# The end of a decoder-layer kernel: a branch decided while the last scatters run, and waits in place of two barriers

## The chip, the cores and the metric

The kernel runs on all eight cores of one Trainium2 chip. The input has eight sequences, and each core computes one of them whole; the cores do not exchange data. The metric is the device time, in microseconds (us), of the slowest core.

## The reference, cut to what matters

The reference is one decoder layer on x of shape (8, 2048, 2048). Three sub-layers add to the residual stream h: a mixer (causal pooling beside an RWKV-7 recurrence), a cross-attention into 256 memory tokens, and a mixture of experts. The last one, and the final norm behind it, are what the end of the kernel computes:

```python
hn = _rmsnorm(h, norm_ffn_g[l])
h = h + _hier_moe(hn, ...)       # top-1 of 4 groups, then top-2 of the 4 experts inside it
return _rmsnorm(h, norm_final_g)
# _hier_moe: for e in range(16):
#     hid = silu(t @ w_gate[e]) * (t @ w_up[e])
#     out = out + gates[:, e:e+1] * (hid @ w_down[e])
```

A token therefore uses two experts of one group, one of the six pairs of that group, and there are 24 such pairs in all.

## The kernel before, in words

The kernel is written as a list of operations per stage. A planner, the class `Sched`, gives each operation a modelled duration and writes them out for five engines in a planned order; `emit` (line 312) turns the order into instructions and places a wait only where an engine does not yet know that an operation is done. Each compute engine has one semaphore that counts its operations. The DMA queues of SP and POOL have 20 semaphores each and use them in turn; each transfer adds 16 to its own.

The stages run in this order: norm and projections, the mixer, cross-attention with the routing of the tokens, and the experts. The expert stage sorts the 2048 tokens of the core into 24 buckets of at most 128 tokens, one for each pair of experts. A bucket is gathered from DRAM by POOL, goes through its two experts, is normed by `finish_bucket`, and is scattered to `out` by POOL with an indirect DMA of 1 MB (line 1395). The last three buckets are finished by expert 15, one after the other: ACT squares the rows, DVE scales them (line 173), POOL issues the scatter.

A bucket holds 128 tokens. If a pair has more, the flag `flgi`, written by DVE before the expert stage begins (line 1305), is 1, and a general path must compute everything once more, tile by tile. The code for it follows the expert stage, inside `with nc.If(fv > 0)` (lines 1459 to 1513). With the present inputs the flag is 0 and the path is skipped: the profile shows none of its compute.

What follows the last scatter, on each of the five engines:

- `S.drain()` (line 1454, the waits themselves on line 372): a wait for every semaphore that is in use, in the order of the list `final`: first the engines' counts, then the DMA semaphores in the order of their first use. There are 43 of them on every engine.
- `nc.all_engine_barrier()` (line 1455): a DRAIN on each engine and an exchange of semaphores through POOL.
- `values_load` (line 1458): each engine loads the flag into a register (TENSOR_LOAD).
- the branch (COMPARE_BRANCH, recorded under line 1513), which jumps over the code of the general path.
- `nc.all_engine_barrier()` (line 1514): a second DRAIN and exchange.

Of the kernel before, what the change touches and what calls it, by code (L numbers as in the profile page):

```python
# [50 lines left out]
class Ring:  # L51
# [3 lines left out]
    def next(self):  # L55
        b = self.b[self.i % len(self.b)]
        self.i += 1
        return b.fresh()
# [9 lines left out]
class Sched:  # L68
# [241 lines left out]
    def emit(self):  # L310
        order = self.schedule()
        self.order = order
        known = {e: {} for e in self.ENG}
        cnt = dict.fromkeys(self.ENG, 0)
        slot_i = dict.fromkeys(self.slots, 0)
        slot_n = {}
        for o in order:
            e = o.eng
            kn = known[e]
            toks = []  # L320
            if o.bytes:
                sl = self.slots[e]
                s = sl[slot_i[e] % len(sl)]
                slot_i[e] += 1
                v = slot_n.get(id(s), (s, 0, None))
                if v[1] > 0:
                    toks.append((v[2].end, s, v[1], v[2].clock))
                slot_n[id(s)] = (s, v[1] + 16, o)
                o.tok = (s, v[1] + 16)
            else:  # L330
                cnt[e] += 1
                o.tok = (self.sem[e], cnt[e])
            for p in o.preds:
                if p.eng == "pe" and e == "pe" and not p.bytes:
                    continue
                toks.append((p.end, p.tok[0], p.tok[1], p.clock))
            toks.sort(key=lambda t: -t[0])
            waits = []
            for _, s, v, ck in toks:
                if kn.get(id(s), 0) >= v:  # L340
                    continue
                waits.append((s, v))
                for k2, v2 in ck.items():
                    if kn.get(k2, 0) < v2:
                        kn[k2] = v2
                if kn.get(id(s), 0) < v:
                    kn[id(s)] = v
            o.clock = dict(kn)
            b = self.b[e]
            if o.pre:  # L350
                for p in o.pre[1]:
                    if p is not None:
                        b.wait_ge(*p.tok)
                o.pre[0](b)
            for s, v in waits[1:]:
                b.wait_ge(s, v)
            r = o.fn(b)
            if not isinstance(r, list):
                r = [r]
            if waits:  # L360
                r[0]._wait_ge(*waits[0])
            r[-1].then_inc(o.tok[0], 16 if o.bytes else 1)
        self.final = [(self.sem[e], cnt[e]) for e in self.ENG if cnt[e]] + [(s, v) for s, v, _ in slot_n.values()]
        self.ops = []

    def all_sems(self):
# [36 lines left out]
def r3(ap, a):  # L403
    return ap.rearrange("p (a b) -> p a b", a=a)
# [19 lines left out]
def build(stop=99, fallback=True):  # L424
    nc = bass.Bass("TRN2", target_bir_lowering=False)  # L425
# [40 lines left out]
    with ExitStack() as es:  # L466
        S = Sched(nc, es)
# [14 lines left out]
        run, tab, tabi, idx, flg, flgi = al.f32(24), al.f32(72), al.f32(48), al.f32(24), al.f32(1), al.f32(1)  # L482
# [30 lines left out]
        def pvc(name, j=0):  # L513
            c = PV[name] + j
            return pv.a[:, c:c + 1]
# [205 lines left out]
        order = [(q, h) for h in range(6) for q in (0, 1)] + [(0, 6), (0, 7), (1, 6), (1, 7), (2, 0), (2, 1), (3, 0), (3, 1)]  # L721
# [244 lines left out]
        if stop >= 2:  # L966
# [7 lines left out]
            for u in range(32 + 2):  # L974
# [7 lines left out]
                if u < 32:  # L982
# [10 lines left out]
                    if u == 0:  # L993
                        for f_ in first:
                            s_, e_, _ = next(r for r in S.regions if r[2] is f_)
# [297 lines left out]
        if stop >= 5:  # L1293
# [126 lines left out]
            for e in range(16):  # L1420
# [14 lines left out]
                for db, j in [(db, j) for db in range(4) for j in range(3)] if e < 15 else [(db, j) for j in range(3) for db in range(4)]:  # L1435
# [5 lines left out]
                    y, yq, _ = bk[b]  # L1441
# [9 lines left out]
                        finish_bucket(b)  # L1451

        S.emit()
        S.drain()
        nc.all_engine_barrier()
        if stop >= 5 and fallback:

            fv = nc.values_load(flgi.a[0:1, 0:1], min_val=0, max_val=1, skip_runtime_bounds_check_because="a comparison gives 0 or 1")
            with nc.If(fv > 0):
                with nc.Fori(0, NTT) as it:  # L1460
                    S2 = Sched(nc, es, "f", dict(sp=4, pool=4, act=1))
                    bank2 = Ring([Buf(psum[:, i * 512:(i + 1) * 512]) for i in range(8)])
                    f_ = Al(S2, big, CONST_W, WORDS)
                    y, xn, XT, gt, hid, sb = f_.f32(D), f_.bf16(D), f_.bf16(D), f_.f32(16), f_.bf16(512), f_.bf16(128)
                    fst, gF2 = f_.f32(8), f_.f32(D)
                    fwr = f_.bf16s(4, 8192)
                    S2.dma("sp", y.a, h2_s[bass.ds(it * 128, 128), :], W=[y])
                    S2.dma("sp", gt.a, gat_s[bass.ds(it * 128, 128), :], W=[gt])
                    S2.dma("sp", gF2.a, gB[3], W=[gF2])

                    def frms():
                        S2.act(xn.a, y.a, AF.Square, R=[y], W=[xn], P=[fst], accum_out=fst.a[:, 0:1])
                        S2.act(fst.a[:, 1:2], fst.a[:, 0:1], AF.Ln, R=[fst], W=[fst], scale=1.0 / D, bias=pvc("epsn"))
                        S2.act(fst.a[:, 2:3], fst.a[:, 1:2], AF.Exp, R=[fst], W=[fst], scale=-0.5)
                    frms()
                    S2.stt(xn.a, y.a, fst.a[:, 2:3], gF2.a, ALU.mult, ALU.mult, R=[y, fst, gF2], W=[xn])
                    for q in range(4):
                        b = bank2.next()
                        S2.mm([(b.a[:, j * 128:(j + 1) * 128], xn.a[:, (q * 4 + j) * 128:(q * 4 + j + 1) * 128], identb.a, True, True) for j in range(4)], R=[xn], W=[b])
                        S2.cp(r3(XT.a, 16)[:, q * 4:q * 4 + 4, :], r3(b.a, 4), R=[b], P=[XT])  # L1480
                    for e in range(16):
                        ws = []
                        for k in range(3):
                            w = fwr.next()
                            for c in range(4):
                                S2.dma("pool", w.a[:, c * 2048:(c + 1) * 2048], wel[k][e][c], P=[w])
                            ws.append(w)
                        for f in range(4):
                            fs = slice(f * 128, (f + 1) * 128)
                            bs = [bank2.next(), bank2.next()]  # L1490
                            for i in range(2):
                                S2.mm([(bs[i].a[:, 0:128], ws[i].a[:, f * 2048 + kc * 128:f * 2048 + (kc + 1) * 128], r3(XT.a, 16)[:, kc, :], kc == 0, kc == 15) for kc in range(16)],
                                      R=[ws[i], XT], W=[bs[i]])
                            S2.act(sb.a, bs[0].a[:, 0:128], AF.Silu, R=[bs[0]], W=[sb])
                            S2.tt(hid.a[:, fs], bs[1].a[:, 0:128], sb.a, ALU.mult, R=[bs[1], sb], W=[hid])
                        for db in range(4):
                            b = bank2.next()
                            ds_ = slice(db * 512, (db + 1) * 512)
                            S2.mm([(b.a, hid.a[:, f * 128:(f + 1) * 128], ws[2].a[:, db * 2048 + f * 512:db * 2048 + (f + 1) * 512], f == 0, f == 3) for f in range(4)], R=[hid, ws[2]], W=[b])
                            S2.stt(y.a[:, ds_], b.a, gt.a[:, e:e + 1], y.a[:, ds_], ALU.mult, ALU.add, R=[b, gt, y], W=[y])  # L1500
                    frms()
                    S2.dma("sp", gF2.a, gB[2], W=[gF2])
                    S2.stt(y.a, y.a, fst.a[:, 2:3], gF2.a, ALU.mult, ALU.mult, R=[y, fst, gF2], W=[y])
                    S2.dma("sp", out[bass.ds(it * 128, 128), :], y.a, R=[y])
                    S2.emit()
                    S2.drain()
                    nc.all_engine_barrier()
                    nums = sorted(s.num for s in S2.all_sems())
                    assert nums[-1] - nums[0] == len(nums) - 1
                    nc.gpsimd.dma_reset(range(nums[0], nums[-1] + 1))  # L1510
                    nc.gpsimd.sem_clear(range(nums[0], nums[-1] + 1))
                    nc.all_engine_barrier()
            nc.end_ifs() if hasattr(nc, "end_ifs") else None
            nc.all_engine_barrier()
    mybir.codegen_inst_isa_subclasses(nc)
    return nc

# [75 lines left out]
```

## Time and profile before

| what | us |
|---|---|
| median of 3 runs | 2406.62 (2404.75 to 2407.84) |
| the profiled execution's own time | 2419.8 |
| its span, first to last recorded instruction, slowest core (core 5) | 2418.2 |
| spans of the other cores | 2385.5 to 2407.6 |

The profile is one execution on the slowest core. The own time is longer than the span, since it also holds what runs ahead of the first recorded instruction and behind the last; no view lists what that is. Times in the rows are counted from the start of the span of their core.
### The profile page before, as it was taken

To read this page: it belongs to the slowest core of one execution; us is meant where nothing else is said; L and a number is where in the kernel's file an instruction comes from. 1 tells how busy PE (TensorE), PEld (TensorE's weight loads), DVE (VectorE), ACT (ScalarE), POOL (GpSimd) and SP (SyncE) were. 2 spreads that over 40 slices of the span, in tenths; PEclk is the share of its full clock that TensorE was granted. 3 is DMA by queue.
4 is the path that set the end of the run, shared out by engine and by line. 5 is a ranking of instruction groups with operands and counts; after the bars stand their busy time and mean duration, and the time that the engine had idled before them with its cause. 6 is when DMAs were issued, how large, how long until landed. Compare 5 with 4: busy or idle time off the path is not lost.

```text
span 2418.2 us, 57666 instructions; the slowest of 8 cores (2385.5 to 2418.2 us)
## 1 busy us (share of the span) xinstructions
PE 2214.5 (92%) x25176; PEld 1264.0 (52%) x25180; DVE 1401.7 (58%) x2734; ACT 1249.3 (52%) x2325; POOL 382.8 (16%) x655
## 2 busy tenths in 40 slices
PE   5899999999889999989997999999999699999995
PEld 3455555555455555545554444455454566655562
DVE  3455667677647666657676334334343567767664
ACT  6655766668677676657776223233232425243333
POOL 3122112221231212311010000000000101111111
PEclk9788999999989999999999999999999699999997
DMA  9689878885886988956775689999999588999983
GB/s 231 98 133 124 107 113 129 128 128 100 138 143 128 151 129 130 141 99 109 121 119 180 145 159 156 160 158 158 167 163 193 184 235 266 284 284 272 278 241 135
DMA packets 178432, 393.80 MB, mean 163 GB/s; under 512 B 59104, under 2 KB 108768, under 8 KB 166400
## 3 DMA queue, kind: packets, MB, share of 16 engines
q0 software_dynamic: 95568, 217.45, 58.0%
q1 hardware_dynamic: 82608, 172.62, 23.3%
q8 instruction: 200, 3.28, 0.6%
q14 instruction: 56, 0.46, 0.1%
HBM read 531.76 MB, written 142.74 MB: 279 GB/s over the span
## 4 chain that ended last, share of the span: by engine, by line
PE 74%; DMA 11%; DVE 7%; ACT 5%; issue 3%; POOL 0%; another core or an unknown queue 0%; POOLq 0%
PE ps L134 74%; ACT big L161 5%; DVE big L168 4%; DVE big L173 2%; DMA big<-wgc 2%; DMA qkd<-big 2%; DMA big<-x 1%; DMA big<-w_kv 1%; DMA big<-w_rkv 1%; DMA big<-w_lo 1%; DMA vod<-big 1%; DMA big<-w_qT 1%; DMA big<-wuc 1%; DVE big L189 1%; DMA big<-h_s,big 1%
## 5 line engine op out<-in xcount | busy, mean ns | idle before, releaser
L134 PE MATMUL ps<-big 64*64 64x64 bf16 (+7 forms) x25176 | 2214.5, 258 | 176.3 <-ACT big L161 69.0
L134 PEld LDWEIGHTS ps<-big 64*64 64x64 bf16 (+3 forms) x25176 | 1263.6, 108 | 1120.2 <-issue 169.3
L161 ACT ACTIVATE big<-ps 128x512 bf16<-128x512 f32 (+2 forms) x922 | 512.4, 591 | 533.5 <-PE ps L134 488.9
L161 ACT ACTIVATE big<-big 128x512 f32<-128x512 f32 (+6 forms) x896 | 546.0, 634 | 432.2 <-DVE big L168 195.2
L168 DVE TENSOR_TENSOR big<-ps,big 128x512 bf16<-128x512 f32 (+3 forms) x664 | 466.2, 714 | 485.7 <-PE ps L134 330.2
L161 ACT ACTIVATE big<-ps,big 128x512 f32<-128x512 f32 (+3 forms) x332 | 213.1, 648 | 179.6 <-PE ps L134 175.6
L173 DVE SCALAR_TENSOR_TENSOR big<-ps,big 128x512 f32<-128x512 f32 (+1 forms) x316 | 224.2, 721 | 107.5 <-ACT big L161 68.4
L173 DVE SCALAR_TENSOR_TENSOR big<-big 128x512 f32<-128x512 f32 (+3 forms) x284 | 237.7, 859 | 32.6 <-ACT big L161 9.8
L168 DVE TENSOR_TENSOR big<-big 128x512 bf16<-128x512 f32 (+12 forms) x412 | 197.7, 503 | 25.5 <-ACT big L161 24.4
L173 DVE SCALAR_TENSOR_TENSOR big<-big,ps 128x64 f32<-128x64 f32 (+1 forms) x280 | 92.6, 332 | 148.1 <-PE ps L134 146.5
L189 DVE CAST big<-ps 128x512 bf16<-128x512 f32 x150 | 100.5, 685 | 31.6 <-ACT big L161 13.0
L203 POOL DMA_DIRECT2D big<-w_kv x128 | 67.9, 539 | 137.8 <-PE ps L134 137.2
L203 POOL DMA_DIRECT2D wuc<-wu_l x64 | 33.5, 523 | 332.5 <-DVE big L168 157.0
L203 POOL DMA_DIRECT2D wdc<-wd_l x64 | 33.7, 527 | 304.6 <-DVE big L168 143.5
L203 POOL DMA_DIRECT2D big<-wg_l x32 | 17.9, 560 | 306.1 <-PE ps L134 306.1
L1230 DVE RECIPROCAL big<-big 128x4 f32<-128x4 f32 x16 | 2.8, 175 | 108.8 <-ACT big L161 108.8
L1395 POOL DMA_INDIRECT out<-big x24 | 30.1, 1254 | 128.2 <-DVE big L173 125.8
L749 DVE TENSOR_TENSOR_SCAN big<-big 128x512 f32<-128x512 bf16 x32 | 39.1, 1221 | 16.3 <-ACT big L161 16.0
L161 ACT ACT_TABLE_LOAD x37 | 47.5, 1283 | 1.7 <-PEq L425 1.1
L203 POOL DMA_DIRECT2D wgc<-wg_l x32 | 16.7, 523 | 191.1 <-DVE big L168 66.2
L203 POOL DMA_DIRECT2D big<-w_o x64 | 34.1, 546 | 73.8 <-PE ps L134 73.4
L203 POOL DMA_DIRECT2D big<-w_rkv x48 | 25.7, 537 | 123.3 <-PE ps L134 122.8
(26 smaller groups left out, 284.5 us busy)
## 6 DMA issues: line engine op xcount, KB each, us to landing
big<-x SPq DMA_DIRECT2D x32, 1024.0 KB, 12.4
wuc<-wu_l POOLq DMA_DIRECT2D x64, 512.0 KB, 10.2
wdc<-wd_l POOLq DMA_DIRECT2D x64, 512.0 KB, 10.4
big<-wuc SPq DMA_DIRECT2D x64, 512.0 KB, 9.4
big<-wdc SPq DMA_DIRECT2D x64, 512.0 KB, 12.9
big<-w_rkv POOLq DMA_DIRECT2D x48, 512.0 KB, 11.8
big<-w_kv POOLq DMA_DIRECT2D x128, 128.0 KB, 5.4
wgc<-wg_l POOLq DMA_DIRECT2D x32, 512.0 KB, 12.6
```

What stands on the lines that cost most here:

```text
L134: r.append(e.matmul(out, lhsT=lhsT, rhs=rhs, start=st, stop=sp_, **k))
L161: return self.op("act", lambda e: e.activation(out=out, in_=in_, func=func, **kw), dur, R, W, P, tbl=TBL.get(func))
L168: return self.op(eng, lambda e: e.tensor_tensor(out=out, in0=a, in1=b, op=op), dur, R, W, P, after=after)
L173: return self.op(eng, lambda e: e.scalar_tensor_tensor(out=out, in0=a, scalar=s, in1=b, op0=op0, op1=op1), dur, R, W, P)
L189: return self.op(eng, lambda e: e.tensor_copy(out=out, in_=a), dur, R, W, P)
L203: return self.op(eng, lambda e: e.dma_start(out=out, in_=in_, **extra), 550.0 if eng == "pool" else 60.0, R, W, P, nbytes=nb, **kw)
L749: S.op("dve", lambda e: e.tensor_tensor_scan(out=tC.a, data0=rmask.a, data1=tS.a, initial=0.0, op0=ALU.mult, op1=ALU.add), 1260.0, R=[rmas ...
L1230: S.op("dve", lambda e, st=st: e.reciprocal(out=st.a[:, 8:12], in_=st.a[:, 4:8]), 100.0, R=[st], P=[st])
L1395: S.op("pool", lambda e: e.indirect_dma_start(out=out, out_offset=IOA(ap=idx.a[:, b:b + 1], axis=0), in_=y.a, in_offset=None, bounds_check ...
```

## The change: what it does

The list `final` is sorted by the time at which the planner expects the last operation behind each semaphore to end. The waits and the barrier ahead of the branch are moved into the general path. In their place each engine waits for the operation that wrote the flag, loads the flag and branches. Behind the branch, in place of the second barrier, stands `S.drain()`: the same 43 waits on every engine, now in the sorted order. Nothing else differs.

```diff
@@ emit
-        self.final = [(self.sem[e], cnt[e]) for e in self.ENG if cnt[e]] + [(s, v) for s, v, _ in slot_n.values()]
+        fin = [(max(o.end for o in order if o.eng == e and not o.bytes), self.sem[e], cnt[e]) for e in self.ENG if cnt[e]]
+        fin += [(o.end, s, v) for s, v, o in slot_n.values()]
+        self.final = [(s, v) for _, s, v in sorted(fin, key=lambda t: t[0])]
@@ build, behind the expert stage
         S.emit()
-        S.drain()
-        nc.all_engine_barrier()
         if stop >= 5 and fallback:
+            for e in S.ENG:
+                S.b[e].wait_ge(*flgi.w.tok)
             fv = nc.values_load(flgi.a[0:1, 0:1], ...)
             with nc.If(fv > 0):
+                S.drain()
+                nc.all_engine_barrier()
                 with nc.Fori(0, NTT) as it:
...
             nc.end_ifs() if hasattr(nc, "end_ifs") else None
-            nc.all_engine_barrier()
+        S.drain()
```

## Rows read from the trace of the kernel before

**Rows 1.** The page: its head, and busy time of the engines.
```profile
span 2418.2 us, 57666 instructions; the slowest of 8 cores (2385.5 to 2418.2 us)
PE 2214.5 (92%) x25176; PEld 1264.0 (52%) x25180; DVE 1401.7 (58%) x2734; ACT 1249.3 (52%) x2325; POOL 382.8 (16%) x655
```

**Rows 2.** Timeline from 2398 us to the end: start, duration, engine, line, operation.
```profile
2396.22 2.35 DVE L173 SCALAR_TENSOR_TENSOR big<-big 128x2048 f32<-128x2048 f32 x1 [0.37 <-ACT big L161]
2398.85 0.98 POOL L1395 DMA_INDIRECT out<-big  x1 [1.75 <-DVE big L173]
```

**Rows 3.** Line 1395 from 2390 us on, the last three scatters: issue to landing.
```profile
DMA to landing us min/median/max: 4.6/4.6/4.6
```

**Rows 4.** Line 372, waits ahead of the first barrier: ns min/median/max, first and last start.
```profile
L372 PEldq EVENT_SEMAPHORE  x43: 51/51/51, 2390.8 to 2405.5; - x43
L372 ACTq EVENT_SEMAPHORE  x43: 13/17/21, 2396.0 to 2404.5; - x43
L372 DVEq EVENT_SEMAPHORE  x43: 21/21/21, 2396.2 to 2404.7; - x43
L372 POOLq EVENT_SEMAPHORE  x43: 4/17/17, 2398.6 to 2404.6; - x43
```

**Rows 5.** Line 372 from 2403.42 us on, behind the last landing.
```profile
L372 POOLq EVENT_SEMAPHORE  x20: 17/17/17, 2403.4 to 2404.6; - x20
L372 DVEq EVENT_SEMAPHORE  x20: 21/21/21, 2403.4 to 2404.7; - x20
L372 PEldq EVENT_SEMAPHORE  x20: 51/51/51, 2403.4 to 2405.5; - x20
```

**Rows 6.** Line 1455, the first barrier: POOL on core 5.
```profile
L1455 POOLq EVENT_SEMAPHORE  x2: 17/17/17, 2413.1 to 2413.1; - x2
L1455 POOLq DRAIN  x1: 8394/8394/8394, 2404.6 to 2404.6; - x1
```

**Rows 7.** Line 1455 on core 0.
```profile
L1455 POOLq DRAIN  x1: 8394/8394/8394, 2371.9 to 2371.9; - x1
```

**Rows 8.** Line 425, the barrier at the start of the program.
```profile
L425 POOLq DRAIN  x1: 188/188/188, 0.6 to 0.6; - x1
```

**Rows 9.** Stretches of core 5: engines' busy time, clock, share of the DMA engines, GB/s.
```profile
2398.90:2403.50 4.60, 0.00 (x0) 0.00 (x0) 0.00 (x0) 0.00 (x0) 0.93 (x1) 0.50 0.45 185
2404.70:2413.10 8.40, 0.00 (x0) 0.00 (x0) 0.00 (x0) 0.00 (x0) 0.00 (x0) 0.50 0.00 0
```

**Rows 10.** Line 1458, the loads of the flag.
```profile
L1458 POOLq TENSOR_LOAD <-big x1: 502/502/502, 2413.2 to 2413.2; - x1
L1458 DVEq TENSOR_LOAD <-big x1: 545/545/545, 2413.3 to 2413.3; - x1
L1458 PEldq TENSOR_LOAD <-big x1: 318/318/318, 2413.4 to 2413.4; - x1
```

**Rows 11.** Line 1513, the branches.
```profile
L1513 PEldq COMPARE_BRANCH  x1: 3402/3402/3402, 2413.7 to 2413.7; - x1
L1513 ACTq COMPARE_BRANCH  x1: 45/45/45, 2413.8 to 2413.8; - x1
L1513 POOLq COMPARE_BRANCH  x1: 53/53/53, 2413.8 to 2413.8; - x1
L1513 DVEq COMPARE_BRANCH  x1: 72/72/72, 2413.9 to 2413.9; - x1
```

**Rows 12.** Line 1514, the second barrier: the first instruction behind the jump.
```profile
L1514 ACTq DRAIN  x1: 43/43/43, 2414.2 to 2414.2; - x1
L1514 PEldq DRAIN  x1: 38/38/38, 2417.2 to 2417.2; - x1
L1514 POOLq DRAIN  x1: 67/67/67, 2417.7 to 2417.7; - x1
L1514 DVEq DRAIN  x1: 10/10/10, 2417.9 to 2417.9; - x1
```

**Rows 13.** DMA queues from 2413.2 to 2418.2 us: packets, MB, share of the engines.
```profile
q14 instruction: 4, 0.03, 2.6%
q8 instruction: 2, 0.03, 2.6%
```

## The prediction, made before the changed kernel ran

> **What bounds the kernel now.** The page says that TensorE is busy for 92% of the span [rows 1]. The change touches none of that: every instruction up to the last scatter stays, in the same order. So the whole question is the stretch from the last scatter to the end, and I read it there, first in the timeline (where does work stop?), then line by line for the sequencers' own instructions, which the timeline leaves out.
>
> The reader should see a chain of five links on core 5. DVE ends the last bucket at 2398.6, and POOL's scatter starts at 2398.85 [rows 2]. It lands 4.6 us later, at 2403.45 [rows 3]; that is the last useful event. Behind it every engine still walks through 20 waits that were long met: until 2404.6 on POOL, 2405.5 on TensorE [rows 5]. Then POOL alone sits in a DRAIN of 8.39 us, from 2404.6 to 2413.0, while four engines wait for it in the barrier [rows 6]. In that time no DMA engine moves anything [rows 9]. Then come the flag (0.5 us, [rows 10]), the branch, and a gap: POOL branches at 2413.8 and goes on at 2417.7, DVE from 2413.9 to 2417.9, TensorE holds its branch for 3.4 us; ACT needs only 0.4 us [rows 11, 12]. In the gap the instruction queues fetch 0.06 MB [rows 13], so those three engines wait for code at the jump's target. The second barrier closes at 2418.2. From landing to the end: 14.75 us in which nothing is computed. Another 1.6 us lie outside the span (own time 2419.8 less 2418.2).
>
> **The change, part by part.** All times are core 5's, in the profiled execution.
>
> *Sorted waits.* The last scatter's semaphore comes late in the list, so its landing is followed by about one wait in place of 20. One wait takes 1.2 us / 19 = 0.063 us on POOL, 0.068 on DVE, 0.11 on TensorE [rows 5].
>
> *Flag and branch early.* Each engine does them once its own last instruction is handed over; these are the first starts of the waits in [rows 4]. The wait for the flag adds 0.06 to 0.11 us (one wait, as above) and holds nobody, since DVE wrote the flag before the expert stage. TensorE: 2390.8 + 0.1 + 0.32 + 3.4 = 2394.6, then 43 waits at 0.11, 2399.3. DVE: 2396.2 + 0.1 + 0.55 + 4.0 = 2400.85, then 43 at 0.068, 2403.8. ACT: 2396.0, a load of about 0.5, and either 0.4 or, should its longer skipped code push the target away, 4.0 us, then 43 waits of about TensorE's price at most: 2401.6 to 2405.2. SP issues nothing here and is earlier. POOL is the last: 2398.6 + 0.06 + 0.50 + 0.05 = 2399.2, code 3.9 [rows 11, 12], 2403.1, then 43 waits at 0.063 = 2.7: **2405.8**. That is 2.4 us behind the landing: on POOL the scatter hides the load and most of the jump, but not the waits.
>
> *POOL's code beside the scatter.* Before, the fetch ran on idle DMA engines; now it runs while the scatter keeps them 45% busy [rows 9]. Bounds: 0, and 4.3 us if no code came before the landing at 2403.45. The nearest row is the quiet gap itself, whose packets need 2.6% of the engines [rows 13]; I take 0.4, and keep both ends for the range.
>
> *Second barrier.* Its exchange, 0.3 us from DVE's arrival at 2417.9 to the end of the span [rows 12, 1], goes.
>
> *First barrier with the DRAIN.* This decides the size. If the 8.39 us are gone, the program's last instruction is at 2405.8 + 0.4 = 2406.2, and 2418.2 - 2406.2 = 12.0 us are saved. But is it the barrier's cost, or a debt of POOL that the first DRAIN pays, wherever it stands? The rows speak for a debt. The duration is 8394 ns on core 5 and on core 0 [rows 6, 7], the first and the last to end of eight cores that all show this figure, and no DMA engine moves anything in its whole length [rows 9]; so it waits for no transfer. POOL's DRAIN before any DMA takes 188 ns [rows 8], the one right after the long one 67 ns [rows 12]. So it is work of fixed size that has piled up over POOL's transfers and is done once. The changed program has no DRAIN. But whatever ends the measured time has to find all engines done, and the way in which this program's own barriers find that is a DRAIN on each engine [rows 8, 12]. If one stands there for POOL, 8.39 us come in place of the 0.07 or so that it costs now: 12.0 - 8.3 = **3.7 us** saved. I take this: the cost follows POOL's transfers, not the line 1455.
>
> The Trainium skill bears on that ("VectorE: DVE Perf Modes", section "The DRAIN you can't avoid"): it knows boilerplate DRAINs of about 12 ns "on all 5 engines, from the preamble/postamble". By its figure the one behind the program costs nothing and the gain would be the 12.0 us of the rival below; by the 8394 ns of [rows 6] it need not be 12 ns for POOL, and no row here shows that stretch.
>
> So: own time 2419.8 - 3.7 = 2416.1 for the profiled execution. It lies 13.2 us above the median of the runs; the tail's length does not depend on what the core did before, so the same difference goes off the median: 2406.6 - 3.7 = **2402.9**.
>
> **The rivals.**
>
> *The DRAIN is really gone* (nothing behind the program drains POOL, or not at that price). Gain 12.0 us, 2394.6; with bounds 0 to 4.3 for the fetch, 8.1 to 12.4, 2394.2 to 2398.5. For it: no row shows a DRAIN behind the program, and the whole stretch outside the span is 1.6 us. Against it: the figure's independence from the place, as above; 1.6 us are what is left once the debt is paid, so they say nothing on who would pay it.
>
> *POOL does not get ahead.* The change claims that the branch is decided while the last scatter runs. On POOL, which issues that scatter, the load of the flag could be held until the scatter's descriptors are done. At the latest, from the landing: 2403.45 + 0.5 + 3.95 + 2.7 = 2410.6, and with the DRAIN behind it 2418.9: 0.7 us later than the span's end now: 2407.3, no change. For it: the scatter occupies POOL for 0.98 us [rows 2]. Against it: POOL's waits begin at 2398.6, before the scatter starts [rows 4, 2], so its sequencer runs ahead.
>
> *A second code fetch on POOL (the slower side).* Behind the jump stand 43 waits where a handful of barrier instructions stood. If they cross into a block of code that is not there, POOL stops once more for the price of a jump, 3.9 us, and everything behind is in series with it: waits, then the DRAIN. This mechanism turns the sum once fetches add more than 3.7 us to POOL's chain, and the change is slower by over 0.2% from 8.5 us on. With one more fetch at 3.9, and the first one held until the landing (4.3 in place of 0.4): 2402.9 + 3.9 + 3.9 = 2410.7. For it: the fetch after the jump is dear on three engines [rows 11, 12]. Against it: the 20 waits of today on POOL follow one another in 1.2 us without such a gap [rows 5], and 2.7 us of waits give a fetch ahead some time. The Trainium skill ("Runtime: NRT & Kernel Launch", section "Instruction fetch mechanics") says that code comes in blocks of 256 instructions and in straight order is mostly hidden. By that rule 43 waits cross a block in about one case in six (an estimate, 43/256), and mostly at no cost.
>
> **How the numbers follow.** Chances: DRAIN paid behind the program 0.55; DRAIN gone 0.32; POOL not ahead 0.07; second fetch 0.06. The likeliest one gives 2402.9; its own range is 2401 to 2407 (2402.5 to 2406.8 by 0 to 4.3 for the fetch, the low end widened by the scatter of the runs, about 1.5). The range of 8 in 10 must hold the two first cases: from 2393 (2394.6 less the scatter of the runs) to 2407.5 (no gain). A measurement of this kernel can tell about 0.2%, 4.8 us, from no change. The first case is below that by 1.1 us, so about 0.2 of it counts as faster; with all of the second, 0.43. Slower: most of the last case and a little noise, 0.05. Within 0.2%: 0.52.
>
> **What would show each step.** In the changed profile, POOL's waits of line 372 should start near 2403 and end 2 to 3 us behind the last landing, on that core's scale; TensorE's branch should still hold 3.4 us, but some 22 us earlier than now, soon after its last matmul; no DRAIN of line 1455. The span should shrink by about 12 us in both main cases. They part in the stretch outside it: 1.6 us as now means that the DRAIN is gone; about 10 us means that it is paid there. The prediction is wrong if that stretch stays short, if POOL's load starts only behind its scatter, or if a second gap stands among POOL's waits.

## The result, and the profile after

The changed kernel takes 2393.18 us (median), the kernel before 2405.68 us in the runs beside it: ratio 0.9947, 95% interval 0.9927 to 0.9968. That is 12.5 us less, and between 7.7 and 17.6 us by the interval. The forecast was 2402.9 us with 3.7 us saved. The rival "the DRAIN is really gone" gave 2394.6. The range of 2393 to 2407.5 holds the result only at its lower end, which was put there for that rival.

The profiled execution took 2392.61 us; its slowest core is core 3. The head of its page, and the busy time of TensorE, PEld, DVE, ACT and POOL:

```profile
span 2391.4 us, 57649 instructions; the slowest of 8 cores (2348.7 to 2391.4 us)
PE 2201.7 (92%) x25176; PEld 1258.7 (53%) x25180; DVE 1402.1 (59%) x2734; ACT 1248.6 (52%) x2325; POOL 381.1 (16%) x655
```

Spans of different executions differ by tens of us from core to core before the end is reached, so they are no measure for the change. What compares is the stretch from the start of the last scatter to the end of the span. Before, it is 2418.2 - 2398.85 = 19.3 us [rows 1, 2], and 19.1 to 19.5 us on all eight cores. The timeline of core 3 after (start, duration, engine, line, operation):

```profile
2381.46 2.35 DVE L173 SCALAR_TENSOR_TENSOR big<-big 128x2048 f32<-128x2048 f32 x1 [0.37 <-ACT big L161]
2384.09 0.98 POOL L1398 DMA_INDIRECT out<-big  x1 [1.75 <-DVE big L173]
```

Now 2391.4 - 2384.09 = 7.3 us, and 7.2 to 7.9 us on the eight cores: about 11.7 us less on average (19.27 to 7.58). The time outside the span is 1.2 us, where it was 1.6. These 11.7 us lie well inside the 7.7 to 17.6 us by which the time fell, so the tail is enough to explain the difference.

How the tail runs now. The loads of the flag (line 1461), then the branches (line 1518), on core 3; columns as in [rows 10, 11]:

```profile
L1461 PEldq TENSOR_LOAD <-big x1: 319/319/319, 2372.0 to 2372.0; - x1
L1461 DVEq TENSOR_LOAD <-big x1: 740/740/740, 2381.5 to 2381.5; - x1
L1461 POOLq TENSOR_LOAD <-big x1: 695/695/695, 2383.9 to 2383.9; - x1
```

```profile
L1518 PEldq COMPARE_BRANCH  x1: 3392/3392/3392, 2372.4 to 2372.4; - x1
L1518 ACTq COMPARE_BRANCH  x1: 45/45/45, 2382.0 to 2382.0; - x1
L1518 DVEq COMPARE_BRANCH  x1: 72/72/72, 2382.3 to 2382.3; - x1
L1518 POOLq COMPARE_BRANCH  x1: 53/53/53, 2384.6 to 2384.6; - x1
```

POOL loads the flag at 2383.9, before its scatter starts at 2384.09: its sequencer does run ahead, and the rival "POOL does not get ahead" is out. The load takes 0.70 us where it took 0.50 [rows 10], and about 1.1 us on four of the cores. The 43 waits behind the branch (line 375), first all of them, then those that start from 2386 to 2389.5 us, then those from 2389.5 us on:

```profile
L375 PEldq EVENT_SEMAPHORE  x43: 51/51/51, 2375.8 to 2389.6; - x43
L375 ACTq EVENT_SEMAPHORE  x43: 17/17/17, 2382.4 to 2389.6; - x43
L375 DVEq EVENT_SEMAPHORE  x43: 21/21/21, 2386.9 to 2391.3; - x43
L375 POOLq EVENT_SEMAPHORE  x43: 17/17/17, 2387.5 to 2391.0; - x43
```

```profile
L375 DVEq EVENT_SEMAPHORE  x33: 21/21/21, 2386.9 to 2389.1; - x33
L375 POOLq EVENT_SEMAPHORE  x33: 17/17/17, 2387.5 to 2389.4; - x33
```

```profile
L375 POOLq EVENT_SEMAPHORE  x10: 17/17/17, 2390.4 to 2391.0; - x10
L375 DVEq EVENT_SEMAPHORE  x10: 21/21/21, 2390.7 to 2391.3; - x10
```

TensorE and ACT are through at 2389.6, when the scatter has landed. POOL and DVE are not: both stop after 33 waits, POOL for 1.0 us (2389.4 to 2390.4), DVE for 1.6 us, and end at 2391.0 and 2391.3.

That is one of two patterns. On cores 1, 3, 5 and 7 POOL stops for about 1.0 us and DVE ends the span. On cores 0, 2, 4 and 6 POOL's first wait comes 4.1 us behind its branch where core 3 needs 2.9, POOL stops for only 0.4 us among the waits, and POOL ends the span. POOL's branch and waits on core 4, whose last scatter starts at 2378.29:

```profile
L1518 POOLq COMPARE_BRANCH  x1: 53/53/53, 2379.2 to 2379.2; - x1
L375 POOLq EVENT_SEMAPHORE  x43: 17/17/17, 2383.3 to 2386.2; - x43
```

On core 3 again: the last scatter, issue to landing (line 1398), and the instruction queue from 2388 us to the end (packets, MB, share of the DMA engines):

```profile
DMA to landing us min/median/max: 5.5/5.5/5.5
```

```profile
q14 instruction: 2, 0.02, 1.2%
```

The landing takes 5.5 us where it took 4.6 [rows 3]. The two instruction packets of this window are the only traffic beside the end of the scatter. They run from 2388.8 to 2389.2, ahead of POOL's stop; while both engines stand, from 2389.4 on, no packet moves. If the later of the two is POOL's (the record does not say whose they are), POOL goes on 1.2 us and DVE 1.6 us behind the end of its packet. Behind the branch, too, POOL's first wait comes 1.1 us and DVE's 1.5 us behind the end of an instruction packet. So the stop is probably a wait for code, like the gap behind the branch.

What the reader should see: the 8.39 us of POOL's DRAIN [rows 6] appear nowhere. No DRAIN stands behind the last wait, and what lies outside the span has not grown.

### The profile page after: what moved, and what is told of

The parts are those of the page before. It is cut to its first block, busy times and chain, and to the rows that moved or that the text cites. A ratio compares the mean times of both kernels' runs of the same rounds, so it can differ in the third digit from the quotient of the medians.

```text
span 2391.4 us, 57649 instructions; the slowest of 8 cores (2348.7 to 2391.4 us)
## 1 busy us (share of the span) xinstructions
PE 2201.7 (92%) x25176; PEld 1258.7 (53%) x25180; DVE 1402.1 (59%) x2734; ACT 1248.6 (52%) x2325; POOL 381.1 (16%) x655
## 4 chain that ended last, share of the span: by engine, by line
PE 75%; DMA 10%; DVE 7%; ACT 5%; issue 2%; POOL 0%; POOLq 0%; DVEq 0%
PE ps L134 75%; ACT big L161 5%; DVE big L168 3%; DVE big L173 3%; DMA qkd<-big 1%; DMA big<-x 1%; DMA big<-w_lo 1%; DMA big<-w_rkv 1%; DMA big<-w_kv 1%; DMA big<-w_qT 1%; DMA big<-h_s,big 1%; DMA big<-wgc 1%; DMA big<-wdc 1%; DVE big L189 1%; DMA out<-big 0%
## 5 line engine op out<-in xcount | busy, mean ns | idle before, releaser
L189 DVE CAST big<-ps 128x512 bf16<-128x512 f32 x150 | 100.6, 685 | 30.4 <-PE ps L134 12.9
L189 DVE COPY big<-big 128x1 f32<-128x1 f32 (+4 forms) x316 | 43.9, 155 | 2.3
```

The lines of the kernel that those rows point to most:

```text
L189: return self.op(eng, lambda e: e.tensor_copy(out=out, in_=a), dur, R, W, P)
```

## The experiments

All of them are read by the same measure, the stretch from the last scatter's start to the end of the span, which varies by about 1 us between cores; times over all runs vary by several us and tell only the largest steps apart.

**Is the long DRAIN a debt?** The kernel before, without its first barrier (line 1455):

```diff
         S.emit()
         S.drain()
-        nc.all_engine_barrier()
         if stop >= 5 and fallback:
```

> The kernel before, without the barrier between the 43 waits and the load of the flag; the barrier behind the branch stays. Theory A (debt): the 8.39 us are work that the first DRAIN on POOL behind its transfers does, wherever it stands. Then the DRAIN of the last barrier, 67 to 103 ns before, takes about 8.4 us, and the time falls by no more than the barrier's exchange, 0.2 us: ratio to before 0.999 to 1.000. Theory B (place): the 8.39 us belong to a DRAIN close behind the last scatter. Then the DRAIN of the last barrier, some 5 us later, stays under 0.2 us and the time falls by about 8.6 us, ratio 0.9964.

Ratio to before 1.000 (0.9965 to 1.0036). The DRAIN of the last barrier on POOL (line 1513), on the slowest core and then on core 0:

```profile
L1513 POOLq DRAIN  x1: 8422/8422/8422, 2405.4 to 2405.4; - x1
```

```profile
L1513 POOLq DRAIN  x1: 8457/8457/8457, 2400.1 to 2400.1; - x1
```

What took 67 to 103 ns behind the long DRAIN takes 8.42 to 8.46 us without it. The stretch is 18.3 us on average, 1.0 less than before, where theory A allowed 0.2: POOL's code behind the branch came in 2.9 to 4.2 us where it had taken 3.8 to 4.1, and the rest of the difference was not taken apart. On the DRAIN theory A holds: of the two DRAINs, the first one pays.

**Does it stay a debt in the changed kernel?** One DRAIN on POOL as the last instruction:

```diff
         S.drain()
+        nc.gpsimd.drain()
```

> The changed kernel with one DRAIN on POOL as its last instruction. Theory A (debt, which the end of the program does not collect by itself): the DRAIN takes 8.39 us and the stretch from the last scatter to the end grows from 7.2 to 7.9 us to about 15.8 us on every core; ratio to before about 0.9984. Theory C (the debt is settled in the background once POOL has been jumping and waiting, or is paid outside the recorded stretch in the changed kernel): the DRAIN is short, under 0.3 us, and the ratio stays near 0.995.

```profile
L1520 POOLq DRAIN  x1: 8398/8398/8398, 2415.2 to 2415.2; - x1
```

8398 ns on all eight cores; the stretch grows to 15.5 to 16.3 us, that is by 8.4 us (16.0 against 7.6 on average). Ratio to before 0.9994 (0.9963 to 1.0025), which fits the 0.9984 of theory A and is too wide to prove it; the row does. This is in effect the kernel that my forecast described. Nothing settles the debt in the background. In the changed kernel nothing inside the measured time pays it: no long DRAIN stands in its span, and only 1.2 us lie outside.

**What is the debt made of?** Two DRAINs, one of them ahead of a scatter, one at the end. The scatter of bucket 0, then of buckets 20 and 12:

```diff
+                def scatter(e):
+                    if b == 0:
+                        e.drain()
+                    return e.indirect_dma_start(out=out, ...)
...
         S.drain()
+        nc.gpsimd.drain()
```

> The changed kernel with two DRAINs on POOL: one ahead of the first scatter, when POOL has issued about 588 of its 651 transfers, and one as its last instruction. If the price of a DRAIN grows with the transfers since the one before (8.39 us / 651 = 12.9 ns each), the last one takes about 63 x 12.9 ns = 0.8 us and the first one at least 7.6 us (more where it also waits for transfers in flight). If the price is fixed once there was any transfer, both take 8.4 us or more and the last one exactly 8.39 us.

> As the kernel with two DRAINs, but the first one ahead of the third-last scatter, so that 3 transfers of POOL lie between the DRAINs. With 63 transfers between, the last DRAIN took 5.2 us, with all 651 of the program 8.4. If the price is per transfer up to a limit (83 ns each below it), the last DRAIN takes 0.25 us and a fixed part of some 0.1. If it is a large fixed part and a small one per transfer (5.4 ns by those two points), it takes 4.9 us.

> The same with 24 transfers between the DRAINs. Per transfer up to a limit: about 2.0 us. Large fixed part: 5.0 us.

The last DRAIN (line 1524) with 63, 3 and 24 transfers of POOL since the one before, one kernel and one profiled execution each; all eight cores of a kernel show the same figure:

```profile
L1524 POOLq DRAIN  x1: 5207/5207/5207, 2407.8 to 2407.8; - x1
```

```profile
L1524 POOLq DRAIN  x1: 298/298/298, 2404.8 to 2404.8; - x1
```

```profile
L1524 POOLq DRAIN  x1: 2022/2022/2022, 2393.4 to 2393.4; - x1
```

From 3 to 24 the price grows by (2022 - 298) / 21 = 82.1 ns a transfer, from 24 to 63 by 81.7. My guess of 12.9 ns (all 651 transfers alike) missed, and so did a price fixed once there was any transfer. A line of 52 ns + 81.9 ns a transfer goes through all three points; 8394 ns is then 102 transfers. The kind of transfer does not matter: the 3 are scatters, the 24 are 12 scatters, 3 gathers and 9 loads of weights, the 63 are 24, 15 and 24. Nor is it the time since the first DRAIN (16, 169 and 423 us on these cores): it would give 11.3 ns a us between the first two and 12.5 between the last two, and it differs between cores that show the same figure. So the price is per transfer, and, if the line holds that far, it stops growing near 100 of them; where exactly, no run shows.

These transfers had all landed. The first DRAIN of the three kernels, with transfers still in flight, took 9.6 to 11.6, 11.0 to 11.1 and 18.9 to 26.2 us; how much of that is waiting for them, the rows don't part.

**What are the parts worth?** The sorted waits alone, on the kernel before:

```diff
-        self.final = [...] + [(s, v) for s, v, _ in slot_n.values()]
+        fin = [...]
+        fin += [...]
+        self.final = [(s, v) for _, s, v in sorted(fin, key=lambda t: t[0])]
```

> The kernel before with the sorted list of waits and nothing else of the change. The DRAIN of the first barrier should start on POOL 0.1 us behind the last landing in place of 1.2 us, and the stretch from the last scatter to the end should shrink from 19.1 to 19.5 us by 1.1 us to about 18.2 us. If another engine's waits end later than POOL's, less.

```profile
L1457 POOLq DRAIN  x1: 8394/8394/8394, 2405.0 to 2405.0; - x1
```

The scatter started at 2400.53 here; the DRAIN starts 4.5 us later, where it was 5.8. The stretch is 18.0 to 18.3 us: 1.1 us saved, as expected.

The change without its early branch: sorted waits, no barriers, but the waits still ahead of the flag. The edit is shown against the kernel with the sorted waits alone:

```diff
         S.emit()
         S.drain()
-        nc.all_engine_barrier()
...
             with nc.If(fv > 0):
+                nc.all_engine_barrier()
...
-            nc.all_engine_barrier()
```

> Neither barrier, sorted waits, but the waits stay ahead of the flag and the branch, and nothing follows the branch: the change without its early branch. The stretch from the last scatter to the end should be landing 4.5 + 0.1 + load 0.5 to 0.7 + branch and code 4.0, but with no instruction left behind the branch to be recorded, the last recorded one is a branch: 5.2 us on POOL, or about 8.6 on TensorE, which holds its branch for 3.4 us. If the early branch is worth what the sum says, the stretch to the end of TensorE's branch is 1 us longer than the changed kernel's 7.2 to 7.9. If code comes faster when four engines ask at once, it is not.

```profile
2377.69 0.97 POOL L1397 DMA_INDIRECT out<-big  x1 [1.75 <-DVE big L173]
```

```profile
L1515 PEldq COMPARE_BRANCH  x1: 3402/3402/3402, 2382.7 to 2382.7; - x1
L1515 POOLq COMPARE_BRANCH  x1: 53/53/53, 2382.8 to 2382.8; - x1
```

The stretch is 8.4 to 8.9 us, 8.6 on average: 1.0 us longer than in the changed kernel. Instruction packets still come behind the end of the span, and the time outside it is 2.3 us (2388.42 - 2386.1). By stretch and outside together, each from its profiled execution's slowest core: before 20.9, sorted waits 19.6, no barriers 10.7, early branch 8.5. The barriers with the DRAIN are 8.9 us of it, the sorted waits 1.3, the early branch 2.2; each figure rests on one execution.

**What holds the end now?** The changed kernel again, and beside it the waits on SP alone:

> The changed kernel itself, beside the next three. Every theory expects the stretch from the last scatter to the end at 7.2 to 7.9 us, as in its first profile, no DRAIN on POOL at the end, and a ratio to before of about 0.995. A ratio of 0.998 or more would say that the gain of the first measurement came from elsewhere.

```diff
-        S.drain()
+        for s, v in S.final:
+            nc.sync.wait_ge(s, v)
```

> The changed kernel, with the 43 waits at the end on SP alone; the four other engines end with their branch. In the changed kernel SP is past its last wait 5.2 to 5.6 us after the last scatter's issue, POOL and DVE only at 6.9 to 7.9, behind a second gap among their waits. Theory: that gap is a second code fetch that only the length of the wait list causes. Then the stretch from the last scatter to the end falls from 7.2 to 7.9 us to 5.5 us or less, the landing itself comes earlier than 5.4 us if the second fetch was what delayed it, and the ratio is about 0.001 lower than that of the changed kernel. Rival: the other engines need the time anyway for what follows the program; then the recorded stretch shrinks, but what lies behind the span grows by the same 2 us and the time stays.

The changed kernel repeats: 7.3 to 8.0 us, ratio 0.9963 (0.9938 to 0.9988) in this set of runs, where the kernel before took 2420.52 us. With SP alone, the last scatter of the slowest core, and SP's waits:

```profile
2398.30 0.98 POOL L1398 DMA_INDIRECT out<-big  x1 [1.75 <-DVE big L173]
```

```profile
L1520 SPq EVENT_SEMAPHORE  x43: 17/17/17, 2367.3 to 2403.8; - x43
```

The stretch is 5.5 to 5.6 us on every core, 2.0 us less than the changed kernel's; the span ends with the landing itself. Outside it are 1.25 us (2405.05 - 2403.8), so nothing is given back. The ratio is 0.9947 (0.9925 to 0.9968) beside 0.9963: below the kernel before, and below the changed kernel by 2 us in the trace, which is less than the runs can tell. The part of the expectation on the landing missed: it stays at 5.5 us. So neither the 43 waits nor the gap among them delayed it. The second fetch itself is not excluded: with SP alone an instruction packet still runs at 2403.1, ahead of the landing, though no engine waits for it any more.

**Why does the scatter land later?** One engine at a time decides late:

```diff
             for e in S.ENG:
                 S.b[e].wait_ge(*flgi.w.tok)
+            S.b["pool"].wait_ge(*S.final[-1])
```

> The changed kernel, but POOL waits for its last scatter to land before it loads the flag. Theory X (code fetches of POOL and DVE take turns with the scatter on a few DMA engines, and that is why it lands 5.2 to 5.5 us after issue in place of 4.5): without POOL's two fetches it lands at about 5.0. Theory Y (POOL's own load and branch hold up the scatter that it is issuing): it lands at 4.5. Under both, the stretch to the end grows to about 4.9 + 0.5 + 4.0 + 43 x 0.061 = 12 us, with a second gap of 1 us.

> The same with DVE in place of POOL. Theory X: without DVE's fetches the scatter lands at about 5.0. Theory Y: it lands at 5.2 to 5.5, as in the changed kernel. The stretch to the end grows to about 5.0 + 0.55 + 4.0 + 43 x 0.069 = 12.5 us, with a second gap of 1 to 1.6 us.

Issue to landing with POOL late, then with DVE late:

```profile
DMA to landing us min/median/max: 5.5/5.5/5.5
```

```profile
DMA to landing us min/median/max: 5.2/5.2/5.2
```

Theory Y falls: with POOL's load and branch out of the way, the scatter still lands at 5.5 us. Theory X expected 5.0 for both and got 5.5 and 5.2, so its sum fails too. What the trace's landing events show is the 16 steps by which the scatter's semaphore rises, probably one for each of the 16 DMA engines. In the kernel before all 16 come by 4.6 us. In the changed kernel 13 do, and three come at 4.8 to 5.5; with POOL or DVE late it is two; with all branches late, none. Fetches of code on those few DMA engines are the likely cause; which fetch costs how much stays open.

The stretch grew as expected, to 11.6 to 11.9 us with POOL late and 12.0 to 12.3 with DVE late. The second gap of the late engine did not come out: it is 0.4 us in both, on every core, where 1.0 and up to 1.6 were expected.

## Why the prediction was wrong, step by step

*The step that failed* is the last of "First barrier with the DRAIN": "If one stands there for POOL, 8.39 us come in place of the 0.07 or so that it costs now: 12.0 - 8.3 = 3.7 us saved. I take this". The first half of that part was right. The 8.39 us are a debt of POOL's transfers, and any first DRAIN pays it, be it 5 us later or at the very end. But I took it for granted that the end of the measured time would call it in, and no row said so. It does not: 1.2 us lie outside the span, where I had written about 10, and the tail became 11.7 us shorter in place of 3.7. The 1.6 us outside the span of the kernel before could not decide it, since there the debt is paid inside; a run without the DRAIN could. That it is "work of fixed size" was wrong as well: the price is 298 ns for 3 transfers, and 8394 ns only looked fixed because 651 transfers lie beyond the point where it stops growing.

The sentence of the Trainium skill that I quoted ("VectorE: DVE Perf Modes", section "The DRAIN you can't avoid", about 12 ns on all 5 engines) led to the right sum. The runs agree in that no long DRAIN stands behind the program, and no run shows its 12 ns.

*The size of the rival was right, by compensation.* It had the program's end 12.0 us earlier; the average over the cores is 11.7. It put POOL's last wait 7.35 us behind the start of the scatter (2406.2 - 2398.85); measured are 6.9 us on core 3, where DVE ends the span at 7.3, and 7.9 on core 4. On core 3 POOL's code took 2.9 us (2384.6 to 2387.5) instead of 4.3, and the gap of 1.0 us came on top, for which I had only a chance of 0.06 ("a second code fetch on POOL") at 3.9 us. On core 4 the code took 4.1 us and the gap 0.4, but the branch came 0.6 us later than written. The landing, 5.5 us in place of 4.6, did not matter to the sum, since POOL's waits end behind it either way.

*A second code fetch* is there on every core, on POOL and on DVE, with 0.4 to 1.0 and 1.2 to 1.6 us instead of 3.9; that the gap is a wait for code is likely by its place behind the packets, not shown by a run of its own. The Trainium skill's rule ("Runtime: NRT & Kernel Launch", section "Instruction fetch mechanics") is that code in straight order is mostly hidden. If the gap is code, it was not hidden here, 33 waits behind a jump.

*POOL is the last* held on half the cores. On the others it is DVE, at 7.2 to 7.3 us: its code took 4.6 us (2382.3 to 2386.9, where I used 4.0), while the scatters were moving, and its gap of 1.6 us came on top.

*Sorted waits, second barrier, flag and branch on TensorE* came out as written: 1.1 us for the waits, the exchange gone, and TensorE's 3.4 us hidden entirely. TensorE even branches 11.7 us ahead of the scatter, where the sum had 7.6: the first wait of [rows 4] was not yet the moment at which its sequencer was free.

*Slower* had no case: on no core does the chain of jump, waits and gap end more than 2.7 us behind the landing.

## What to carry to other kernels

The barrier at the end of this kernel, which issues 651 transfers from POOL, contained a DRAIN of 8.4 us: look at the sequencer's rows, not at the timeline, which doesn't show it. Semaphore waits for the last stores did what the barrier did, without that price, and one engine that had nothing else to do could hold them for all. When a cost is found to be a debt, ask next whether anyone in the measured time collects it. In the kernel that still pays it, the time outside the span doesn't tell; in the one that no longer does, it is the bound.

## What the runs showed of the hardware that was not expected

- POOL's DRAIN costs 52 ns + 82 ns for each of POOL's transfers since the last one, though they have all landed: 298 ns for 3, 2022 for 24, 5207 for 63; at 651 it is 8394 ns, the price of about 102.
- The landing of the 1 MB scatter came 0.7 to 1.1 us later while instruction packets ran beside it: three of the 16 steps of its semaphore were late, none where no engine jumped before the landing.
- The same jump costs very unequal times: 0.4 us from branch to first wait on ACT, 2.7 to 4.9 us on POOL, DVE and TensorE over the eight cores of the changed kernel.
